# One instruction of 2048 columns in place of two of 1024 for each gathered row, in the value stage of a hybrid diffusion block

## What is computed

```python
def one_chunk(args):
    hc, ic, gc = args
    u_sel = u[ic]
    act = jax.nn.gelu(jnp.einsum('cd,ced->ce', hc, u_sel))
    wts = (gc * act.astype(jnp.float32)).astype(v.dtype)
    return jnp.einsum('ce,ced->cd', wts, v[ic])
```

## Time and profile before

| | us |
|---|---|
| median of 3 runs | 2186.73 |
| lowest, highest | 2185.06, 2189.71 |
| the profiled execution | 2179.53 |
| its span, first to last instruction | 2177.7 |
| value stage in it, from its first split tile to the closing matmuls | about 1556 to 2148 |

### The profile page before, as it was taken

One profiled execution on the slowest core, in us unless ns is written; L12 is line 12 of the kernel. 1 busy time (PEld: TensorE's weight loads), 2 busy tenths in 40 slices (PEclk: granted clock), 3 DMA queues, 4 the chain that ended last, 5 costly groups with the idle time before them and its releaser, 6 DMA issues.

```text
span 2177.7 us, 42186 instructions
## 1 busy us (share of the span) xinstructions
PE 2089.6 (96%) x13442; PEld 1848.0 (85%) x13442; DVE 1674.4 (77%) x2955; ACT 1223.7 (56%) x2243; POOL 310.3 (14%) x264
## 2 busy tenths in 40 slices
PE   3899999899999999999999999999999999999997
PEld 0478888667999999999999999999888778788786
DVE  5377767697666478878878588778688898988986
ACT  2332234486344477677776555655566666666664
POOL 0000000000000000000000211111334564322320
PEclk7899999899999999999999999999999999999999
DMA  9878876500565545555589644445689999999991
GB/s 385 336 282 284 280 261 234 189 1 1 205 243 190 172 155 186 180 182 184 183 294 365 210 157 161 154 157 183 244 306 363 357 358 347 334 364 354 389 337 69
DMA packets 160909, 524.75 MB, mean 241 GB/s; under 512 B 34976, under 2 KB 35792, under 8 KB 160208
## 3 DMA queue, kind: packets, MB, share of 16 engines
q1 hardware_dynamic: 123840, 452.63, 58.2%
q0 software_dynamic: 20576, 67.20, 8.9%
q10 hardware_dynamic: 16432, 4.19, 0.9%
HBM read 515.52 MB, written 8.39 MB: 241 GB/s over the span
## 4 chain that ended last, share of the span: by engine, by line
PE 88%; DVE 5%; DMA 4%; issue 1%; ACT 1%; SPq 0%; DVEq 0%; ACTq 0%
PE PS L790 71%; PE PS L1103 9%; DMA raw<-stream 2%; PE PS L1047 2%; DMA ada_t<-w_ada 2%; PE PS L946 1%; DVE st L1341 1%; PE PS L920 1%; PE PS L833 1%; DVE w_lo L1140 1%; PE PS L797 1%; PE PS L773 1%; PE PS L934 1%; ACT w_hi L438 1%; DVE mixed L1662 0%
## 5 line engine op out<-in xcount | busy, mean ns | idle before, releaser
L438 ACT ACTIVATE w_hi<-raw 128x512 fp32r<-128x512 f32 x1088 | 683.3, 630 | 691.9 <-PE PS L790 552.2
L1140 DVE TENSOR_TENSOR w_lo<-raw,w_hi 128x512 fp32r<-128x512 f32 x1088 | 734.1, 690 | 337.1 <-ACT w_hi L438 321.4
L790 PE MATMUL PS<-h_h,w_hi 128*128 128x256 f32 (+1 forms) x2304 | 658.1, 286 | 3.1 <-DVE h_l L1170 2.1
L790 PE MATMUL PS<-h_h,w_lo 128*128 128x256 f32 (+1 forms) x2304 | 653.1, 283 | 0.0
L790 PE MATMUL PS<-h_l,w_hi 128*128 128x256 f32 (+1 forms) x2304 | 653.0, 283 | 0.0
L790 PEld LDWEIGHTS PS<-h_h,w_hi 128*128 128x128 f32 x2304 | 443.4, 192 | 4.2 <-issue 2.6
L790 PEld LDWEIGHTS PS<-h_l,w_hi 128*128 128x128 f32 x2304 | 443.5, 193 | 0.0
L790 PEld LDWEIGHTS PS<-h_h,w_lo 128*128 128x128 f32 x2304 | 443.1, 192 | 0.0
L790 PE MATMUL PS<-w_hi,p_hl 128*128 128x512 f32 x1024 | 400.1, 391 | 7.3 <-DVE w_lo L1140 7.0
L790 PEld LDWEIGHTS PS<-w_hi,p_hl 128*128 128x128 f32 x1024 | 192.6, 188 | 51.5 <-issue 10.9
L1103 PE MATMUL PS<-w_hi,p_hl 128*128 128x512 f32 x512 | 199.8, 390 | 0.0
(11 more groups left out here) (228 smaller groups left out, 2834.0 us busy)
## 6 DMA issues: line engine op xcount, KB each, us to landing
raw<-stream SPq DMA_DIRECT2D x544, 512.0 KB, 4.0
raw_far<-stream SPq DMA_DIRECT2D x104, 512.0 KB, 6.8
ada<-w_ada SPq DMA_DIRECT2D x96, 512.0 KB, 4.4
ada_t<-w_ada SPq DMA_DIRECT2D x64, 512.0 KB, 9.3
ada_u<-w_ada SPq DMA_DIRECT2D x32, 512.0 KB, 5.6
values_scratch<-A ACTq DMA_DIRECT2D x1, 2560.0 KB, 19.0
x_c<-x_ctx SPq DMA_DIRECT2D x1, 2048.0 KB, 7.6
x<-x_lat SPq DMA_DIRECT2D x1, 2048.0 KB, 15.0
```

Of the source, the lines that this page charges most:

```text
L438: nc.scalar.activation(w_hi[:, (2 * j + hf) % SPLIT, :], ring[:, j, hf * HALF:(hf + 1) * HALF], ACT.Copy).then_inc(S["w_high"], 1)
L790: ins = mm(out_, l_, r_, start=(start and q == 0), stop=(stop and q == 2), skip_group_check=check)
L1140: V_.tensor_tensor(w_lo[:, h % SPLIT, :], ring[:, h // 2 % RAW, at_:at_ + HALF], w_hi[:, h % SPLIT, :].bitcast(F32), ALU.subtract).then_in ...
```

## The change

Each row is mixed by one instruction over all 2048 columns. In a turn it stands where the first half stood, behind the first four halves; the add behind the second four halves is gone. The row of rounds 3, 4, 8 and 12 that lies behind a turn is one instruction too. It counts 2 on `mixed` at its end (row 0: 4), and the next row waits for that. GpSimd's program, SyncE's, ScalarE's and TensorE's stay as they are.

```diff
--- before.py
+++ after.py
@@ -1653,21 +1653,17 @@
                 V_.tensor_tensor(p_hl[:, s, DENSE:2 * DENSE], A[:, bass.ds(i, 1), 0:DENSE].rearrange("p a t -> p (a t)"),
                                  p_hl[:, s, 0:DENSE].bitcast(F32), ALU.subtract).then_inc(S["p_low"], 1)
 
-            def mix(r, s, hf):
-
-                cols = slice(hf * UNIT, (hf + 1) * UNIT)
-                if hf == 0:
-                    dve.wait_ge(row_in[s], 32 * r + 32)
-                dve.wait_ge(S["mixed"], 8 * r + (2 * s + hf + 1))
-                V_.scalar_tensor_tensor(mixed[:, cols], row_t[:, s, cols], weight[:, bass.ds(4 * r + s, 1)],
-                                        mixed[:, cols], ALU.mult, ALU.add).then_inc(S["mixed"], 1)
-
-            def first_mix(hf):
-
-                cols = slice(hf * UNIT, (hf + 1) * UNIT)
+            def mix(r, s):
+
+                dve.wait_ge(row_in[s], 32 * r + 32)
+                dve.wait_ge(S["mixed"], 8 * r + (2 * s + 2))
+                V_.scalar_tensor_tensor(mixed[:], row_t[:, s, :], weight[:, bass.ds(4 * r + s, 1)],
+                                        mixed[:], ALU.mult, ALU.add).then_inc(S["mixed"], 2)
+
+            def first_mix():
+
                 dve.wait_ge(row_in[0], 32)
-                V_.tensor_scalar(mixed[:, cols], row_t[:, 0, cols], weight[:, 0:1], None, ALU.mult
-                                 ).then_inc(S["mixed"], 3 - 2 * hf)
+                V_.tensor_scalar(mixed[:], row_t[:, 0, :], weight[:, 0:1], None, ALU.mult).then_inc(S["mixed"], 4)
 
             def ring_of(b):
 
@@ -1678,12 +1674,10 @@
                 split_low(b + (98 + b0), 2, ring_of(98 + b0))
                 split_low(b + (98 + b0), 3, ring_of(98 + b0))
                 if add is not None:
-                    add(0)
+                    add()
                 p_low(2 * b + (2 * b0 + 2), 0)
                 split_low(b + (99 + b0), 0, ring_of(99 + b0))
                 split_low(b + (99 + b0), 1, ring_of(99 + b0))
-                if add is not None:
-                    add(1)
                 p_low(2 * b + (2 * b0 + 3), 1)
 
             dve.wait_ge(S["gelu_in"], NE_TILES - 2 * ROUTE_AT + 2)
@@ -1707,13 +1701,12 @@
 
             def four_turns(b, b0, r, first=False):
                 for s in range(4):
-                    value_turn(b, b0 + s, first_mix if first and s == 0 else lambda hf: mix(r, s, hf))
+                    value_turn(b, b0 + s, first_mix if first and s == 0 else lambda: mix(r, s))
 
             def three_turns(b0, r):
                 for s in range(3):
-                    value_turn(0, b0 + s, lambda hf: mix(r, s, hf))
-                mix(r, 3, 0)
-                mix(r, 3, 1)
+                    value_turn(0, b0 + s, lambda: mix(r, s))
+                mix(r, 3)
 
             weights(0)
             four_turns(0, 3, 0, first=True)
```

## The result

The changed kernel took **2207.78 us** (median of 4 runs, 2204.57 to 2210.42), the kernel before 2185.89 (4 runs, 2184.12 to 2189.71): a ratio of 1.0097, 95% interval 1.0078 to 1.0116. It is 1.0% slower, some 21 us; forecast were 2208.3 and +21.6 us. The interval reaches from +17 to +25 us, so that the forecast came out within 1 us of the measured time is luck; that it lies near it is not.

What follows compares the result with a forecast made beforehand. TensorE was taken to bound the value stage, with VectorE close behind. 28.3 + 2.4 - 9.1 = +21.6 us, added to 2186.7, gave 2208.3 us, 1.0% slower; range 2194 to 2219.

Steps and rivals of the forecast that it cites:

- The bound and the cover: Value stage: TensorE sets the pace; VectorE may come back to `w_lo` 0.59 us later before TensorE loses time.
- The mix of 2048: One 2048-column instruction on VectorE takes 2.35 us, 1.07 more than one of 1024.
- 59 turns at 0.48: Turns with a row: TensorE loses 0.48 us behind each turn's first tile, 28.3 us in all.
- The ends of rounds: Rounds 3, 4, 8, 12: the pairs' loss of 9.1 us goes; stalls of 0.48, or 0.67 at round 3, remain.
- the slow matmuls of round 3: End of round 3: ten matmuls at 1.2 GHz cost 1.64 us more, counted within the 9.1 that goes.
- The turn right behind an end: Turns after rounds 3, 4, 8, 12: VectorE not quite caught up, 0.07 us more, four times, 0.3.
- Row 0: First row: the wider `tensor_scalar` adds at most 0.75 us, covered, so 0.
- VectorE's saved work: VectorE over 63 mixes: its work falls by about 14 us, which is hidden.
- the row fetches: GpSimd: fetches start about 3.5 us earlier in the turn, at no cost, 0.
- The weight loads: Raw slots come free up to 1.07 us later; taken as 0, with 3 us for the range.
- The clock rival: Value stage: 63 new gaps of 0.6 us might drop TensorE's clock; at every fourth stall 26 us more, 2234; 8%.
- The rival that merging pays: The 59 turns: a mix holding VectorE under 1.79 us stalls none, gaining 9.1 us, 2177.6; 5%.

Runs made afterwards that it cites:

- first_1536: Kernel before, with a row's two instructions 1536 and 512 columns wide in place of 1024 and 1024: 2177.52 us, ratio 0.9992.
- first_1792: Kernel before, with a row's two instructions 1792 and 256 columns wide in place of 1024 and 1024: 2186.40 us, ratio 1.0038.
- pair_first: Kernel before, with both 1024-column instructions in the first place of each turn, nothing merged: 2210.09 us, ratio 1.0143.
- spread: Kernel before, with the four rows of rounds 3, 4, 8 and 12 spread over six places of their turns, nothing behind the turn: 2171.89 us, ratio 0.9964.
- mid_tile: Changed kernel, with its 2048-column mix moved to the middle of the first tile, ahead of the last two halves: 2178.56 us, ratio 1.0005 to the kernel before.
- late_count: Changed kernel, with the row's second count on `mixed` given in the turn's second place: 2203.64 us, ratio 1.0110 to the kernel before.
- after_again: Changed kernel run once more without any edit: 2198.96 us, ratio 1.0099 to the kernel before.
- ends_only: Kernel before, with only the four rows behind a turn (rounds 3, 4, 8, 12) merged into one 2048-column instruction: 2177.98 us, ratio 0.9999.
- waits_first: Changed kernel, with TensorE's waits at a tile's first half reordered, `p_low` and `p_high_too` ahead, `w_low` last: 2198.00 us, ratio 1.0046 to the kernel before.
- mid_waits: Kernel with the 2048-column mix in mid-tile, plus waits for `p_low` and `p_high_too` on each tile's third half: 2190.94 us, ratio 1.0022 to the kernel before.

## Why the prediction was right, point by point

- **The bound and the cover.** TensorE sets the pace, VectorE has 0.59 us beyond its old stretch at a tile's start. Confirmed from three sides: 0.53 more is free (first_1536), 0.80 more costs 0.21 (first_1792), 1.07 costs 0.48 (the change), 1.19 costs 0.61 (pair_first: 0.53 + 0.08).
- **The mix of 2048.** 2.35 us forecast, 2.344 measured; the stretch grew by 1.07 us (1997.28 to 1999.81 is 2.53, have 1.47).
- **59 turns at 0.48.** They cost what was forecast, 28 us. Each stall stood alone, and each next mix began on time.
- **The ends of rounds.** The four pairs' loss went: 9.1 us in the profile of before, and -8 us when spread alone removed it. (As the prediction writes the sum, 3 x 1.80 + 3.63 is 9.0; the trace gives 9.1.) Whether the 1.64 us for the slow matmuls of round 3 are lost in every execution, one profile of the kernel before can't show: in first_1536 a gap of 2.15 us had none behind it. After the change the gap at round 3 is 0.80 us, at the others 0.54 to 0.60: 0.2 more for `weights`, where 0.19 was forecast. The turn right behind an end was to lose 0.07 more and lost 0.02 to 0.1 less: that TensorE's own restart (0.08) gives VectorE a lead that I had left out would fit, but was not tested. Below 1 us in all.
- **Row 0, VectorE's saved work, the row fetches.** All 0, as forecast; mid_tile and late_count bear on the fetches. The saved work was put too high: 14 us is the sum of durations, which overlap. From start to next start a mix of 1024 costs VectorE 1.20 us and one of 2048 2.26 (1997.28 to 1999.54), so some 8 us were saved. The wide `tensor_scalar` took 1.28 us and no stall followed.
- **The weight loads.** Taken as 0, since TensorE "waits for none of that". That reading was wrong: in the profile of before, TensorE lost 2.0 us between 1574 and 1672 us, mostly behind late weights (11.1 lost in all, 9.1 of it at the ends), and after_again has no such loss. So by the two profiles the change costs 30.1 - 11.1 = 19.0 us in the stage, and by the medians 21.5; the forecast of 21.6 lies inside both measured intervals, but not every term of it is confirmed to the last 2 us.

Here is the worst of them, ScalarE and then TensorE in the kernel before:

```profile
1670.03 1.15 ACT L438 ACTIVATE w_hi<-raw 128x512 fp32r<-128x512 f32 x2 [2.13 <-DMA raw<-stream]
```
```profile
1671.62 0.47 PE L790 MATMUL PS<-w_hi,p_hl 128*128 128x512 f32 x1 [0.27 <-DVE w_lo L1140]
```

- **The clock rival.** With 63 gaps of 0.62 us, 9.5 us apart, TensorE kept 2.4 GHz: matmuls start every 0.227 us ahead of and behind each, and the granted clock of the stage is 1.00. The rule that short idles between groups make the clock go back and forth (the Trainium skill, "TensorE: Matmul & The Clock Gate", the second failure mode) did not hold for gaps of this kind here.
- **The rival that merging pays.** The saving per instruction is real: 1.19 us for a second instruction, 1.07 for its columns added to the first. The Trainium skill ("VectorE: DVE Perf Modes", the TRN2 errata) states such a cost per instruction, and the trace agrees. The saving was worth 0.12 us at four places (ends_only) and nothing at the 59 others.

What I had wrong in the theory came out only in an experiment: I took the cover as one number for every half. The term in it that depends on the place is TensorE's hand-over, the time from the start of `w_lo` to the first matmul: 0.92 us at a tile's start and 0.74 inside. At a tile's start the change sits on the dearer one, and some 10 of its 21 us hang on the order of three waits.

## What to carry to other kernels

When two engines pass buffers through a short ring, ask of an edit how long it keeps an engine away at one stretch, not how much work it saves: here some 8 us of VectorE's time were saved and 21 us lost, and the same columns in smaller stretches were free. Read the cover from a place where the kernel already stalls (delay less loss), and check it in an undisturbed place. On the waiting side, put the wait that comes last directly ahead of the instruction that needs it, and those long satisfied ahead of it.

## What the runs showed that I had not expected

- The wait that ended last, with two more instructions of the queue between it and the matmul, cost TensorE 0.18 us more at a restart than the same wait on the weight load of that matmul (0.92 against 0.74 us from the start of `w_lo`); 0.16 of it reached the second matmul (1.23 against 1.08). Waits long satisfied, on instructions ahead of it, cost nothing that shows.
- The start of the value stage, where GpSimd gathers four rows at once and the DMA engines are fully busy (a share of 1.01 from 1560 to 1570 us), is in part a matter of chance: up to 1600 us TensorE lost 5.6 us in the first profile of the change, 8.0 in waits_first, 6.5 in mid_waits, and at most 1.2 in the nine others, the second profile of the change among them. Here the first of them, VectorE idle for want of weights and then TensorE:

```profile
1567.52 0.69 DVE L1140 TENSOR_TENSOR w_lo<-raw,w_hi 128x512 fp32r<-128x512 f32 x1 [3.51 <-issue]
1571.04 0.69 DVE L1140 TENSOR_TENSOR w_lo<-raw,w_hi 128x512 fp32r<-128x512 f32 x1 [2.82 <-issue]
```
```profile
1568.27 0.50 PE L790 MATMUL PS<-w_hi,p_hl 128*128 128x512 f32 x1 [1.12 <-issue]
...
1571.78 0.59 PE L790 MATMUL PS<-w_hi,p_hl 128*128 128x512 f32 x1 [2.09 <-DVE w_lo L1140]
```

  The gap of 2.47 us was followed by slow matmuls (0.43 us apart, 1.2 GHz), and so were the gaps of 3.9 us in the two others; those of 2.15 and 2.03 us at round 3 (first_1536, ends_only) were not, that of 2.22 (before) was. None of the gaps of 0.6 us was.
